# Latent attention on one Trainium2 core: query product, key products, output product and rotary product change places among the heads

## What is computed

```python
def mla_query(c_q, g_qa, w_qup):
    q = (rms_norm(c_q, g_qa) @ w_qup).reshape(b, t, MLA_HEADS, QK_NOPE + QK_ROPE)
    return q[..., :QK_NOPE], q[..., QK_NOPE:]

def mla_keyvalue(c_kv, g_kva, w_kvup):
    kv = (rms_norm(c_kv, g_kva) @ w_kvup).reshape(b, t, MLA_HEADS, QK_NOPE + V_DIM)
    return kv[..., :QK_NOPE], kv[..., QK_NOPE:]

def dense_attention(q, k, v):
    scale = 1.0 / math.sqrt(QK_NOPE + QK_ROPE)
    s = jnp.einsum('bqhd,bkhd->bhqk', q, k).astype(jnp.float32) * scale
    p = jax.nn.softmax(s, axis=-1).astype(v.dtype)
    return jnp.einsum('bhqk,bkhd->bqhd', p, v)
...
            k_l = assemble_keys(kn_l, kp_l)
            o_lat = latent_attention(q_l, k_l, v_l, k_c, v_c)
            y_lat = (o_lat * jax.nn.silu(p_lat[..., pe_hi:])) @ mla_w_out[idx]
```

## Time and profile before

| | us |
|---|---|
| median of 3 runs | 1366.55 |
| lowest, highest | 1365.65, 1366.65 |
| the profiled execution | 1365.68 |
| its span, first to last instruction | 1363.9 |
| attention's loop within it | 132 to 281 |

### The profile page before, as it was taken

One profiled execution on the slowest core, in us unless ns is written; L12 is line 12 of the kernel. 1 busy time (PEld: TensorE's weight loads), 2 busy tenths in 40 slices (PEclk: granted clock), 3 DMA queues, 4 the chain that ended last, 5 costly groups with the idle time before them and its releaser, 6 DMA issues.

```text
span 1363.9 us, 18081 instructions
## 1 busy us (share of the span) xinstructions
PE 1341.1 (98%) x6873; PEld 1116.2 (82%) x6873; DVE 719.3 (53%) x969; ACT 596.0 (44%) x926; POOL 503.4 (37%) x235
## 2 busy tenths in 40 slices
PE   8999999999999999999999999999999999999998
PEld 4688788789888888877779889888888888888886
DVE  1794777655845338567547265336437244252442
ACT  4554877744433444545655344342343132231331
POOL 0252001145522494412235233254654444444441
PEclk9999999999999999999999999999999999999999
DMA  9962001184322152311223222133324333333331
GB/s 347 320 215 65 1 22 32 42 273 153 89 81 62 32 168 82 95 43 47 62 62 94 77 77 77 47 109 93 93 79 122 93 92 96 104 93 92 101 100 62
DMA packets 206614, 136.05 MB, mean 100 GB/s; under 512 B 10169, under 2 KB 187946, under 8 KB 206554
## 3 DMA queue, kind: packets, MB, share of 16 engines
q1 hardware_dynamic: 206352, 135.18, 32.7%
q10 hardware_dynamic: 202, 0.06, 0.0%
HBM read 130.51 MB, written 4.72 MB: 99 GB/s over the span
## 4 chain that ended last, share of the span: by engine, by line
PE 88%; DVE 5%; ACT 4%; DMA 1%; issue 1%; ACTq 0%; POOL 0%; DVEq 0%; SPq 0%; POOLq 0%
PE psum L2066 28%; PE psum L2068 27%; PE psum L2067 27%; PE psum L2122 2%; ACT probs L930 1%; DMA ada_late<-in_w_ada 1%; ACT probs L935 1%; PE psum L2276 1%; ACT pt_hi L940 1%; PE psum L2518 1%; DVE neg_max L1566 1%; PE psum L2643 1%; PE psum L2216 0%; DVE pt_lo L1559 0%; DVE u_lo L1582 0%
## 5 line engine op out<-in xcount | busy, mean ns | idle before, releaser
L672 POOL TENSOR_TENSOR w_lo<-w_raw,w_hi 128x1024 fp32r<-128x1024 f32 x180 | 441.6, 2457 | 688.4 <-ACT w_hi L782 560.3
L2066 PE MATMUL psum<-u_hi,w_hi 128*128 128x512 f32 (+1 forms) x960 | 368.3, 384 | 1.0 <-DVE u_lo L1582 0.8
L2068 PE MATMUL psum<-u_hi,w_lo 128*128 128x512 f32 (+1 forms) x960 | 360.9, 376 | 0.0
L2067 PE MATMUL psum<-u_lo,w_hi 128*128 128x512 f32 (+1 forms) x960 | 360.9, 376 | 0.0
L782 ACT ACTIVATE w_hi<-w_raw 128x1024 fp32r<-128x1024 f32 x180 | 189.4, 1056 | 206.5 <-PE psum L2068 155.5
L2066 PEld LDWEIGHTS psum<-u_hi,w_hi 128*128 128x128 f32 x960 | 181.2, 189 | 38.0 <-issue 1.6
L2068 PEld LDWEIGHTS psum<-u_hi,w_lo 128*128 128x128 f32 x960 | 181.0, 189 | 33.5
L2067 PEld LDWEIGHTS psum<-u_lo,w_hi 128*128 128x128 f32 x960 | 181.3, 189 | 31.7 <-issue 0.9
L2066 PE MATMUL psum<-y_hi,w_hi 128*128 128x512 f32 x416 | 162.4, 390 | 0.0
L2067 PE MATMUL psum<-y_lo,w_hi 128*128 128x512 f32 x416 | 161.9, 389 | 0.0
L2068 PE MATMUL psum<-y_hi,w_lo 128*128 128x512 f32 x416 | 161.8, 389 | 0.0
(11 more groups left out here) (458 smaller groups left out, 2266.3 us busy)
## 6 DMA issues: line engine op xcount, KB each, us to landing
w_raw<-in_w_in SPq DMA_DIRECT2D x52, 512.0 KB, 3.8
w_raw<-in_w_up SPq DMA_DIRECT2D x32, 512.0 KB, 4.0
w_raw<-in_w_down SPq DMA_DIRECT2D x32, 512.0 KB, 3.6
ada_back<-in_w_ada SPq DMA_DIRECT2D x7, 2048.0 KB, 11.2
w_raw<-in_fno_w_in SPq DMA_DIRECT2D x16, 512.0 KB, 3.8
ada_w<-in_w_ada SPq DMA_DIRECT2D x3, 2048.0 KB, 16.1
w_raw<-in_mla_w_in SPq DMA_DIRECT2D x11, 512.0 KB, 5.4
w_raw<-in_mla_w_out SPq DMA_DIRECT2D x8, 512.0 KB, 3.8
```

The costliest lines, as they stand in the source:

```text
L672: pool.tensor_tensor(WL[:, j, :], RAW[:, j % 2, :], f(WH[:, j, :]), ALU.subtract).then_inc(lo_done, 1)
L2066: pe.matmul(out, ah, bh, start=first, stop=False)
L2067: pe.matmul(out, ah, bl, start=False, stop=False)
L2068: return pe.matmul(out, al, bh, start=False, stop=last)
```

## The change

PE's order in iteration j becomes: scores 2, ROPED (j = 1 only), NOPED, weigh, turn 0, K_LAT, scores 3, K_CTX, turn 1, output, scores 0 of the next head, turn 2, scores 1 of the next head, ROPED of head j + 2 (j = 2 and 4), turn 3. No matmul is added or taken away. K_LAT goes from bank 1 to bank 0, where NOPED and K_CTX are, so K_LAT now waits for NOPED to be taken out, and K_CTX for K_LAT. ACT and DVE get lists to match. On ACT `turned` 1 and 2 go ahead of `scaled` 2 and 3. On DVE the gate's product (`output`) goes behind `inverse` 3, and `output_lo` behind `turned` 2. NOPED goes ahead of ROPED on both.

```diff
@@ units
-            units += [(j + 1, ROPED)] * (j < LAST) + [(j - 1, O_LAT)] * (j > 0) + [(j + 1, u) for u in (NOPED, K_LAT, K_CTX)] * (j < LAST)
+            units += [(j + 1, NOPED), (j + 1, ROPED)] * (j < LAST) + [(j - 1, O_LAT)] * (j > 0) + [(j + 1, u) for u in (K_LAT, K_CTX)] * (j < LAST)
...
-            return bank({NOPED: 4, ROPED: 0, K_LAT: 6}.get(u, 1) if j == 0 else {K_LAT: 1, O_LAT: 1}.get(u, 0))
+            return bank({NOPED: 4, ROPED: 0, K_LAT: 6}.get(u, 1) if j == 0 else {O_LAT: 1}.get(u, 0))
...
-            return sum(1 for x in units[:unit_no(j, u)] if not (x[1] == ROPED and x[0] % 2))
+            n = sum(1 for x in units[:unit_no(j, u)] if not (x[1] == ROPED and x[0] % 2))
+            swapped = j and j % 2 == 0 and u in (NOPED, ROPED)
+            return n + (1 if u == NOPED else -1) if swapped else n
@@ ACT
                 if nxt:
-                    if j % 2:
-                        rope_raw(j + 1)
+                    if j == 1:
+                        rope_raw(2)
+                    unit(j + 1, NOPED)
                     unit(j + 1, ROPED)
                 if j:
                     unit(j - 1, O_LAT)
-                if nxt:
-                    unit(j + 1, NOPED)
                 turned(j, 0)
...
+                turned(j, 1)
                 scaled(j, 2)
-                turned(j, 1)
                 exps(j, 3)
                 if j:
                     output(j - 1)
+                turned(j, 2)
                 scaled(j, 3)
-                turned(j, 2)
                 if nxt:
                     exps(j + 1, 0)
                     scaled(j + 1, 0)
+                if j in (2, 4):
+                    rope_raw(j + 2)
                 turned(j, 3)
@@ DVE
                 top(j, 2)
                 if nxt:
+                    unit(j + 1, NOPED)
                     if j % 2:
                         rope(j + 1)
                     unit(j + 1, ROPED)
                 if j:
                     unit(j - 1, O_LAT)
-                if nxt:
-                    unit(j + 1, NOPED)
                 turned(j, 0)
...
-                if j:
-                    output(j - 1)
                 turned(j, 1)
                 inverse(j, 3)
                 if j:
-                    output_lo(j - 1)
+                    output(j - 1)
                 if nxt:
                     top(j + 1, 0)
                 turned(j, 2)
+                if j:
+                    output_lo(j - 1)
@@ PE
                 elif u == K_CTX and j:
+                    pe.wait_ge(un_lo, unit_no(j, K_LAT))
+                elif u == K_LAT and j:
                     pe.wait_ge(un_lo, unit_no(j, NOPED))
-                elif u == K_LAT and j >= 2:
-                    pe.wait_ge(un_lo, unit_no(j - 2, O_LAT))
...
             def output(j):
-                pe.wait_ge(un_lo, unit_no(j, O_LAT) if j >= LAST - 1 else unit_no(j + 2, K_LAT))
+                pe.wait_ge(un_lo, unit_no(j, O_LAT))
```

More of the change, by code:

```diff
@@ L2308, in _ @@
                 scores(j, 2)
-                if nxt and j % 2:
-                    unit(j + 1, ROPED)
+                if nxt:
+                    if j == 1:
+                        unit(2, ROPED)
+                    unit(j + 1, NOPED)
                 if j:
                     weigh(j - 1)
-                if nxt:
-                    unit(j + 1, NOPED)
                 turn(j, 0)
@@ L2320, in _ @@
                     unit(j + 1, K_CTX)
+                turn(j, 1)
                 if j:
                     output(j - 1)
-                turn(j, 1)
                 if nxt:
@@ L2328, in _ @@
                     scores(j + 1, 1)
+                    if j in (2, 4):
+                        unit(j + 2, ROPED)
                 else:
```

## The result

The changed kernel takes 1372.5 us (median of 6 runs, 1369.5 to 1377.8) where the kernel before takes 1366.5 (median of 6, 1364.9 to 1368.7). The ratio is 1.0047, with a 95% interval from 1.0037 to 1.0058: 6 us slower, 1.3 more than forecast and within the range.

What follows compares the result with a forecast made beforehand. PE, busy 98% of the span, was taken as the bound. Losses of 11.1 us less gains of 5.9 and 0.5 gave +4.7 on 1365.68, 1370.4; the median's 0.87 made it 1371.2 us, range 1368.0 to 1374.0.

Steps and rivals of the forecast that it cites:

- slowed rotation: Rival, chance 0.15: POOL's w_lo overlaps DVE's rotation and splits run slow too, +0.9 to +2.5 us more, 1372 to 1374 us.
- What goes away: PE's waits at turn 2, weighing, turn 3 of iterations 2 and 4, and for o_lat_lo go: 5.9 us gained.
- Turn 3 in iterations 1, 3, 5, 6: PE waits 1.17 us instead of 0.50, as u_hi comes late and holds up pt_hi 2: 2.7 us lost.
- ACT's lateness: ACT running late in attention, a sum of many slots; half of it gone would take 1.5 us off.
- Second key product: K_CTX waits for kn_lo: 0.31 us in even iterations, 1.82 in 3 and 5, 0.8 in iteration 1.
- Head 2's query product: In iteration 1 NOPED waits for the copy qp_raw of the rotary product in the same bank: 1.2 us lost.
- First head: K_LAT waits about 1.6 us for qn_lo, of which 1.0 is given back: net 0.6 us lost.
- Last head: No next head's work covers its waits: 3.9 us against 2.8 before, 1.1 us more.
- Modulation: Behind attention, DVE's 0.34 us wait for the modulation load goes; with the output projection's earlier input, 0.5 us gained.
- Gains win: Rival, chance 0.09: u_hi never holds pt_hi 2 up and ACT never falls late, 3.3 us lost against 6.4 gained, 1363.5 us.
- It cancels out: Rival, chance 0.16: u_hi costs half and rotary heads wait under 1.0 us at K_CTX, +1.6 us, 1368 us.

Runs made afterwards that it cites:

- e3: Changed kernel with DVE's gate product moved ahead of the reciprocal of block 3; median 1366.2 us, ratio 1.000 to the kernel before.
- e5: Changed kernel with DVE's rotation for heads 4 and 6 moved to the end of iterations 2 and 4; median 1369.8 us.
- e8: Changed kernel with the edits of e2, e3 and e5, and head 2's rotary product at the end of iteration 0; median 1361.2 us, ratio 0.9970.
- e6: Changed kernel with ACT's u_hi moved behind the taking out of turn 2; median 1369.8 us.
- e4: Kernel before with only the loop's first key product (head 1, 512 keys) put in bank 0, so that it waits; median 1372.1 us, ratio 1.0037.
- e2: Changed kernel with the loop's first key product (head 1, 512 keys) back in bank 1; median 1371.0 us.
- e9: Changed kernel with the edits of e2 and e3 together; median 1365.5 us, ratio 0.9989 to the kernel before.
- e10: Kernel of e8 with ACT's scaling of head 7's block 0 behind the taking out of turn 3 in iteration 6; median 1361.2 us, ratio 0.9954.
- e7: Changed kernel with the smaller key product (256 keys) in bank 1 instead of bank 0; median 1370.4 us.

## Why the prediction was right

**Direction and size.** Forecast +4.7, measured +6.1 in the medians. In PE's own steps, without the clock, attention with its end gives 6.5 - 1.5 = 5.0. The 1372.5 lies in the forecast's own range (to 1373) and also in that of the slowed rotation (1372 to 1374); the times don't choose between the two, the trace does.

**What goes away.** Confirmed: turn 2 without a wait in iterations 1 to 6 (3.10 after turn 1), turn 3 without one in 2 and 4, weighing of heads 0 to 5 without one above 0.1, no wait for o_lat_lo.

**Turn 3 in iterations 1, 3, 5, 6.** Forecast 1.17 from start to start, measured 1.15 four times. The chain by which it was worked out is the one in the trace, and e3 shows that its first link, the product behind the reciprocal, is the cause: 4.9 us with what hangs on it (turn 3's wait down to 0.4, ACT no longer late, the last head shorter). That this one swap is worth the whole net loss was not said by the forecast; it had put 2.7 on this term and had booked ACT's lateness and the last head apart.

**Second key product.** Even iterations: forecast 0.31, measured 0.30. Iteration 1: 0.8 and 0.75. Iterations 3 and 5: forecast 1.82, measured 1.67 and 1.64. Right in mechanism, and e3, e5 and e8 split it: 0.6 goes with ACT's lateness (e3), 0.8 with the rotation's place (e5), and 0.3 is left with both edits (e8), the price of the shared bank.

**Head 2's query product** behind qp_raw: 1.2 forecast, 1.25 measured. **First head:** the wait 1.6 forecast, 1.64 measured. **Last head:** 3.9 of waits forecast, 3.8 measured. **Modulation:** DVE starts it at 285.86 straight behind pt_lo, without the wait for its load.

**The miss: the clock.** The step on the first head counted the wait and what is given back of it, and took the matmuls behind it at their old pace. They run at the lower level from 138.75 to 142.17 us: three matmuls of the key product and four of the score block take 0.43 instead of 0.23 from start to start. Key product and score block took 4.0 where 2.5 was due, so 1.5 us. With it the forecast would have been 1372.7. In e6's trace, where the clock stayed up, PE is 0.5 behind after this iteration, close to the 0.6 forecast; in the changed kernel 2.0. e4 shows that the wait is enough, e2 that the low clock goes with it. It isn't in every execution: six of the seven traces with that wait have it and e6's doesn't; of the five without the wait (before, e2, e8, e9, e10) none has it at this place.

**Rivals.** "Gains win" is out: u_hi was held up in every iteration (0.82 by the bracket, seven times). "It cancels out" is out too: turn 3 waits the full 1.15 and the second key product of heads 4 and 6 over 1.6. "Slowed rotation" did not occur in the changed kernel, whose rotation starts behind POOL's instruction (0.68 for its first step), but did in e5 and e8 (1.72).

**What stays open.** Single executions of every kernel here, the one before too, are 2 to 9 us longer than the shortest, with a mean clock of 0.991 to 0.997 instead of 0.999. The longest that was traced, the changed kernel's first, has its low clock at 550 to 700 us; e5's trace (0.996) has two short stretches there, at 550 to 600 and at 650 to 700 us, and e7's (0.996) one there and one in the last head. Eight of the twelve traces, that of before among them, are low somewhere between 550 and 600 us, with PE busy all the time ahead of it. What starts it was not tried, and nothing here says why e4's median lies 6.3 us above that of before when its attention loses 2.6.

## What to carry to other kernels

With in-order engines, ask of every instruction that a change moves what now stands ahead of it on its own engine and how late that one is: a 0.68 us product put behind a reciprocal that had to wait cost 5 us over attention's loop, although both were off the critical engine. Order the engines that hand a buffer back so that what frees it comes first. A new wait on the matrix engine can cost more than its length, since the matmuls behind it may run at the lower clock.

## What was not expected of the hardware

- A wait of 1.4 to 2.3 us by the bracket, coming 2 us after one of 0.8, was followed in six of seven traces by six to eight matmuls at half the pace (0.43 instead of 0.23 us for 512 columns); those of 1.0 to 1.5 us in the middle of attention were not. Waits of 1.3 and 0.6 us in the last head were followed by it in one trace (e7: 0.58 granted from 278 to 282 us, 256 columns in 0.21 instead of 0.12) and not in the others. And the clock also fell with no wait ahead of it: in the kernel before, 0.57 between 576 and 580 us.
- A DVE product of 512 fp32 columns that reads no accumulator memory took 0.69 us alone, and 1.14 (before) to 1.72 (e5, e8) where POOL's w_lo ran at its start. Each time it ended 0.54 to 0.55 us behind w_lo (190.32 behind 189.77 in the kernel before, 196.29 behind 195.75 in e5), as if most of it had waited for POOL. One that read the accumulator memory kept its time: the changed kernel's qn_lo at 194.88 us took 0.69, with POOL busy beside 0.58 of it (w_lo, 193.62 to 195.46).
